# Four token blocks of row fetches become two, and the other two go densely through all experts

## The reference

```python
q = (xt @ wq).reshape(t, 8, 2, 128)
sc = jnp.einsum('thkd,hknd->thkn', q, keys)
s1, i1 = lax.top_k(sc[:, :, 0], 16); s2, i2 = lax.top_k(sc[:, :, 1], 16)
top_s, ci = lax.top_k(all sums s1 + s2, 16)
experts = i1[ci // 16] * 128 + i2[ci % 16]      # 8 heads x 16 of 16384 experts per token
gates = softmax(top_s)
act = gelu(einsum('td,thkd->thk', x, u_tab[experts])) * gates
y = einsum('thk,thkd->td', act, v_tab[experts])
```

## Time and profile before

| | before |
|---|---|
| median of 3 runs | 3802.77 us |
| the profiled execution | 3807.15 us |
| its span | 3805.4 us |
| mean granted TensorE clock | 0.85 |
| PE, DVE, POOL busy | 71%, 54%, 49% |
| moved by DMA | 694.02 MB |
| first expert numbers written (L1278) | at 164.00 us |
| last expert sum added (L1323) | at 1986.33 us |

### The profile page before, as it was taken

One profiled execution on the slowest core, in us unless ns is written; L12 is line 12 of the kernel. 1 busy time (PEld: TensorE's weight loads), 2 busy tenths in 40 slices (PEclk: granted clock), 3 DMA queues, 4 the chain that ended last, 5 costly groups with the idle time before them and its releaser, 6 DMA issues.

```text
span 3805.4 us, 40545 instructions
## 1 busy us (share of the span) xinstructions
...
## 2 busy tenths in 40 slices
...
GB/s 172 128 309 301 279 286 334 321 340 259 313 322 333 310 267 345 332 339 341 356 306 34 67 23 1 1 1 1 56 73 95 89 87 59 23 45 78 95 94 78
DMA packets 417984, 694.02 MB, mean 182 GB/s; under 512 B 35784, under 2 KB 280691, under 8 KB 417667
## 3 DMA queue, kind: packets, MB, share of 16 engines
q0 software_dynamic: 147456, 536.94, 39.7%
q1 hardware_dynamic: 270339, 154.50, 13.9%
...
...
## 4 chain that ended last, share of the span: by engine, by line
PE 51%; DVE 16%; POOL 13%; DMA 10%; issue 6%; ACT 3%; SPq 1%; DVEq 0%; ACTq 0%
PE PS L1593 25%; POOL ring L601 13%; DMA ring<-in_peer_v,eidx 7%; PE PS L768 6%; DMA ring<-in_peer_u,eidx 2%; PE PS L747 2%; DVE ring L1301 2%; PE PS L1495 1%; PE PS L1504 1%; PE PS L653 1%; PE PS L1501 1%; DVE X L1316 1%; PE PS L1603 1%; DVE W L1175 1%; PE PS L1615 1%
## 5 line engine op out<-in xcount | busy, mean ns | idle before, releaser
L601 POOL DMA_INDIRECT ring<-in_peer_u,eidx x512 | 635.8, 1242 | 404.0 <-DVE eidx L1278 177.9
L601 POOL DMA_INDIRECT ring<-in_peer_v,eidx x512 | 588.0, 1148 | 351.4 <-PE PS L768 192.1
L1593 PE MATMUL PS<-held_uH,GW 128*128 128x264 f32 (+1 forms) x3648 | 693.1, 290 | 35.9 <-POOL BIG_value L2120 31.8
L1301 DVE CUSTOM_DVE_ANT_0 ring<-ring,hn 128x1024 f32<-128x1024 f32 x512 | 614.7, 1223 | 115.6 <-DMA ring<-in_peer_u,eidx 106.8
L2106 POOL TENSOR_TENSOR GW<-held_wr,GW 128x1024 fp32r<-128x1024 f32 x178 | 428.6, 2409 | 453.2 <-ACT GW L1883 453.2
L768 PE MATMUL PS<-ring,dg 128*128 128x512 f32 x1024 | 528.2, 655 | 172.4 <-DMA ring<-in_peer_v,eidx 168.0
L1593 PEld LDWEIGHTS PS<-held_uH,GW 128*128 128x128 f32 x3648 | 581.7, 193 | 48.9 <-issue 32.4
L1593 PE MATMUL PS<-BIG_value,GW 128*128 128x264 f32 (+1 forms) x1824 | 486.1, 287 | 0.0
L768 PEld LDWEIGHTS PS<-ring,dg 128*128 128x128 f32 x1024 | 196.2, 206 | 460.6 <-DMA ring<-in_peer_v,eidx 276.6
L1316 DVE SCALAR_TENSOR_TENSOR X<-ring,gact,X 128x1024 f32<-128x1024 f32 x256 | 328.6, 1284 | 186.0 <-DMA ring<-in_peer_v,eidx 181.4
L1593 PE MATMUL PS<-hid,GW 128*128 128x264 f32 (+1 forms) x3072 | 370.4, 282 | 0.0
...
## 6 DMA issues: line engine op xcount, KB each, us to landing
held_wr<-in_w_ff SPq DMA_DIRECT2D x128, 512.0 KB, 4.0
wqr<-in_peer_wq SPq DMA_DIRECT2D x64, 512.0 KB
held_wr<-in_w_in_ab SPq DMA_DIRECT2D x18, 512.0 KB, 3.9
ring<-in_peer_u,eidx POOLq DMA_INDIRECT x512
ring<-in_peer_v,eidx POOLq DMA_INDIRECT x512
BIG<-in_w_in SPq DMA_DIRECT2D x4, 1536.0 KB, 11.4
held_wr<-in_w_qkv_c SPq DMA_DIRECT2D x12, 512.0 KB, 3.8
w_out<-in_w_out SPq DMA_DIRECT2D x1, 4096.0 KB, 19.0
```

What stands on the lines that cost most here:

```text
L601: e.indirect_dma_start(out=ring[:, i % RING, :], out_offset=None, in_=rows_u if k < HK else rows_v, in_offset=bass.IndirectOffsetOnAxis(ap ...
L1301: e.tensor_tensor_reduce(row, row, hn[:, :], 1.0, 0.0, ALU.mult, ALU.add, act[:, k:k + 1]).then_inc(*n.up(e_dot))
L1593: ins = e.matmul(bank[b + a][:, 0:w], w_[:, k * P:(k + 1) * P], x_[:, c0:c0 + w], start=(first and z in (0, 2)), stop=(last and z >= 4))
```

## The change

`first_order()` is written anew. All four fronts come first, one after another, and one expert row of block 0 (a `slot`) follows each of their steps as far as its row is known. Then block 2 and 3, together 256 tokens (`TD`), go through all 16384 experts, with no row fetched by its number:

- `prepare` turns the expert numbers of blocks 2 and 3 into two picks of 0 to 127 (`found`, `picks`), and makes the norms `hs` of both blocks again, transposed and split into high and low parts (`h_hl`).
- 64 `group`s of 4 tokens make the table of gates. For each token DVE writes two 128x128 matrices (first pick; second pick times gate), PE multiplies them, and ACT copies the result into a staging buffer. After every 16 groups SP writes 4 MB of the table to memory (`gates_all`), in runs of 64 floats.
- 128 `tile`s follow, one for each second pick. A tile takes 128 rows of each table, 512 KB each (the first from a transposed copy of the table that the host lays out). ACT casts to the high part and POOL (`low_u`) or DVE subtracts for the low part. PE makes 24 products of 256 columns for the scores, ACT the gelu, DVE multiplies with the tile's gates, and PE makes 24 more products into four banks that gather the sum over all tiles.
- The 256 rows of block 1 are slots between the tiles, 3 after each, with all `v` rows on DVE. The tails of blocks 0 and 1 are put between tiles too; those of 2 and 3 come last, as does the loading of the second transformer block's constants.

Semaphores are merged and some constants moved into a ring buffer to make room. The second transformer block keeps its instructions.

```diff
+GATHERED = (0, 1)
+DENSE = (2, 3)
+TD = P * len(DENSE)
+GROUPS = TD // 4
+STAGE = 64
+FIXED = 149
+def gather_order():
+    for blk in GATHERED:
+        yield "begin", blk
+        for k in range(HK):
+            yield "u", blk, k
+        yield "gate", blk
+        for k in range(HK):
+            yield "v", blk, k
+        yield "end", blk
...
+    rows = list(gather_order())
+    rows.reverse()
+    def ready(name):
+        done = taken.get(("front", name[1]), 0)
+        if name == ("begin", 1):
+            return ("tile", 0) in order
+        if name[0] == "begin":
+            return done >= 40
+        if name[0] == "u":
+            return (done - 35) // 5 > name[2] // TOPK
+        return done == FRONT_STEPS
+    def slots(some):
+        while some and rows and ready(rows[-1]):
+            name = rows.pop()
+            order.append(name)
+            if name[0] in "uv":
+                some -= 1
...
+    fronts += [(("front", b), FRONT_STEPS) for b in range(1, NB)]
     while fronts:
         step(fronts)
-    late = []
-    for b in range(3):
-        late += [(("pproj", b), 1), (("tail", b), TAIL_STEPS)]
-    late.append((("pproj", 3), 1))
-    experts(3, late, (4, 4))
+        slots(1)
+    order.append(("prepare",))
+    for j in range(GROUPS):
+        order.append(("group", j))
+        if j % 2:
+            slots(1)
+    while ready(rows[-1]):
+        slots(1)
+    late = [(("tail", 0), TAIL_STEPS)]
+    for f in range(P + 2):
+        order.append(("tile", f))
+        slots(3)
+        if not rows and taken.get(("tail", 1)) is None and (("tail", 1), TAIL_STEPS) not in late:
+            late.append((("tail", 1), TAIL_STEPS))
+        if f > 8 and f % 3 == 0:
+            step(late)
+    while rows:
+        slots(1)
+    order.append(("sum",))
+    order.append(("second",))
+    if (("tail", 1), TAIL_STEPS) not in late and ("tail", 1) not in taken:
+        late.append((("tail", 1), TAIL_STEPS))
     while late:
         step(late)
-    order += [("tail", 3)] * TAIL_STEPS
...
+    for b in DENSE:
+        order += [("tail", b)] * TAIL_STEPS
...
+        for c in range(TD // STAGE):
+            e.wait_ge(p_ev, STAGE // 4 * (c + 1))
+            e.dma_start(gates_all[:, :, STAGE * c:STAGE * c + STAGE].rearrange("f p t -> p f t"), stage[c % 2]).then_inc(d_go[c % 2], 16)
+        e.wait_ge(d_go[0], 16 * (TD // STAGE // 2))
+        e.wait_ge(d_go[1], 16 * (TD // STAGE // 2))
+        for q in range(3):
+            dense_gates(e, q)
...
+        for f in range(2, P):
+            tables(e, f)
+            if f % 2 == 0 and 3 <= f // 2 + 1 < P // 2:
+                dense_gates(e, f // 2 + 1)
+        e.dma_start(met, ap["meta_tokens_2"]).then_inc(d_p, 16)
         e.wait_ge(t_pT, 1)
         e.dma_start(pin[0], piv[3]).then_inc(d_pin, 16)
+        e.wait_ge(e_x, NB)
+        second_loads(e)
+    def tables(e, f):
+        if f >= 2:
+            e.wait_ge(u_lo, f - 1)
+        e.dma_start(raw_u[f % 2], ap["peer_u_turned"][f].rearrange("p k e -> p (k e)")).then_inc(d_u[f % 2], 16)
+        if f >= 2:
+            e.wait_ge(v_lo, f - 1)
+        e.dma_start(raw_v[f % 2], rows_v.rearrange("(p f) d -> f p d", f=P)[f]).then_inc(d_vt[f % 2], 16)
+    def dense_gates(e, q):
+        if q >= 3:
+            e.wait_ge(a_g, 2 * (q - 3) + 2)
+        e.dma_start(g_ring[:, q % 3], gates_all[2 * q:2 * q + 2].rearrange("f p t -> p f t")).then_inc(d_g[q % 3], 16)
...
+    def low_u(e, n, f):
+        if f < P:
+            e.wait_ge(u_hi, f + 1)
+            e.tensor_tensor(r(u_hl[:, f % 2, 1]), raw_u[f % 2], u_hl[:, f % 2, 0], ALU.subtract).then_inc(*n.up(u_lo))
...
+            elif name[0] == "u":
+                gather(e, 256 * name[1] + name[2] + RING)
+            elif name[0] == "v":
+                gather(e, 256 * name[1] + HK + name[2] + RING)
+            elif name[0] == "tile":
+                if name[1] == 0:
+                    low_u(e, n, 0)
+                low_u(e, n, name[1] + 1)
...
+    def group_tensor(e, n, j):
+        e.wait_ge(p_oh, j + 1)
+        if j >= 2:
+            e.wait_ge(p_ev, j - 1)
+        for i in range(4):
+            ins = e.matmul(bank[1 + j % 2][:, i * P:(i + 1) * P], hot1[:, j % 2, i, :], hot2[:, j % 2, i, :], start=True, stop=True)
+        ins.then_inc(*n.up(p_mm))
+    def score_bank(f):
+        return bank[4 + f % 2][:, 0:TD]
+    def tile_tensor(e, n, f):
+        if f < P:
+            e.wait_ge(u_lo, f + 1)
+            if f >= 2:
+                e.wait_ge(a_gelu, f - 1)
+            for k in range(8):
+                hi, lo = (r(u_hl[:, f % 2, a, k * P:(k + 1) * P]) for a in range(2))
+                x_hi, x_lo = (r(h_hl[:, a, k, :]) for a in range(2))
+                e.matmul(score_bank(f), hi, x_hi, start=(k == 0), stop=False)
+                e.matmul(score_bank(f), hi, x_lo, start=False, stop=False)
+                ins = e.matmul(score_bank(f), lo, x_hi, start=False, stop=(k == 7))
+            ins.then_inc(*n.up(s_mm))
+        g = f - 2
+        if g >= 0:
+            e.wait_ge(v_lo, g + 1)
+            e.wait_ge(a_lo, g + 1)
+            a_h, a_l = (r(a_hl[:, g % 2, a, :]) for a in range(2))
+            for c in range(8):
+                hi, lo = (r(v_hl[:, g % 2, a, c * P:(c + 1) * P]) for a in range(2))
+                dst = bank[c // 2][:, TD * (c % 2):TD * (c % 2) + TD]
+                e.matmul(dst, hi, a_h, start=(g == 0 and c % 2 == 0), stop=False)
+                e.matmul(dst, hi, a_l, start=False, stop=False)
+                ins = e.matmul(dst, lo, a_h, start=False, stop=(g == P - 1 and c % 2 == 1))
+            ins.then_inc(*n.up(y_mm))
...
+    def tail_banks(blk):
+        return (6, 7, 7, 7, 6, 6) if blk in GATHERED else (0, 1, 2, 3, 4, 5)
...
+    def group_scalar(e, n, j):
+        c, i = j // (STAGE // 4), j % (STAGE // 4)
+        if i == 0 and c >= 2:
+            e.wait_ge(d_go[c % 2], 16 * (c // 2))
+        e.wait_ge(p_mm, j + 1)
+        e.copy(stage[c % 2][:, :, 4 * i:4 * i + 4], bank[1 + j % 2].rearrange("p (t f) -> p f t", t=4)).then_inc(*n.up(p_ev))
+    def high_u(e, n, f):
+        if f < P:
+            e.wait_ge(d_u[f % 2], 16 * (f // 2 + 1))
+            if f == 0:
+                for c in range(2):
+                    e.wait_ge(d_go[c], 16 * (TD // STAGE // 2))
+            if f >= 2:
+                e.wait_ge(s_mm, f - 1)
+            e.copy(r(u_hl[:, f % 2, 0]), raw_u[f % 2]).then_inc(*n.up(u_hi))
+    def tile_scalar(e, n, f):
+        if f == 0:
+            high_u(e, n, 0)
+        high_u(e, n, f + 1)
+        g = f - 1
+        if 0 <= g < P:
+            e.wait_ge(s_mm, g + 1)
+            if g >= 2:
+                e.wait_ge(a_lo, g - 1)
+            e.activation(a_raw[:, g % 2], score_bank(g), ACT.Gelu).then_inc(*n.up(a_gelu))
+            e.wait_ge(d_vt[g % 2], 16 * (g // 2 + 1))
+            if g >= 2:
+                e.wait_ge(y_mm, g - 1)
+            e.copy(r(v_hl[:, g % 2, 0]), raw_v[g % 2]).then_inc(*n.up(v_hi))
+            e.wait_ge(a_g, g + 1)
+            e.copy(r(a_hl[:, g % 2, 0]), a_raw[:, g % 2]).then_inc(*n.up(a_hi))
...
+    def renew_hn(e, n, blk):
+        if blk:
+            e.wait_ge(*n.next(f_sq))
+            inverse_root(e, n, sm[:, 5:6], sm[:, 4:5], D)
+            e.wait_ge(*n.now(rinv))
+            e.wait_ge(*n.now(e_dot))
+            e.scalar_tensor_tensor(hn[:, :], X[:, blk, :], sm[:, 5:6], gffn2, ALU.mult, ALU.mult).then_inc(*n.up(dve))
...
+    def group_vector(e, n, j):
+        if j == 0:
+            e.wait_ge(p_T, 1)
+        if j >= 2:
+            e.wait_ge(p_mm, j - 1)
+        for i in range(4):
+            t = 4 * j + i
+            e.tensor_scalar(hot1[:, j % 2, i, :], line[:, :], picks[:, 0, t:t + 1], None, ALU.is_equal)
+            ins = e.tensor_scalar(hot2[:, j % 2, i, :], line[:, :], picks[:, 1, t:t + 1], picks[:, 2, t:t + 1],
+                                  ALU.is_equal, ALU.mult)
+        ins.then_inc(*n.up(p_oh))
+    def tile_vector(e, n, f):
+        g = f - 1
+        if 0 <= g < P:
+            q = g // 2
+            e.wait_ge(a_gelu, g + 1)
+            e.wait_ge(d_g[q % 3], 16 * (q // 3 + 1))
+            e.tensor_tensor(a_raw[:, g % 2], a_raw[:, g % 2], g_ring[:, q % 3, g % 2], ALU.mult).then_inc(*n.up(a_g))
+            e.wait_ge(v_hi, g + 1)
+            e.tensor_tensor(r(v_hl[:, g % 2, 1]), raw_v[g % 2], v_hl[:, g % 2, 0], ALU.subtract).then_inc(*n.up(v_lo))
+            e.wait_ge(a_hi, g + 1)
+            e.tensor_tensor(r(a_hl[:, g % 2, 1]), a_raw[:, g % 2], a_hl[:, g % 2, 0], ALU.subtract).then_inc(*n.up(a_lo))
...
+    ut = np.ascontiguousarray(inputs["peer_u"].reshape(P, P, 8, P).transpose(1, 3, 2, 0))
+    arrays["in_peer_u_turned"] = ut
```

618 lines of the change are left out of this document (363 added, 255 removed).

## The result

The changed kernel takes 4448.35 us, the median of 4 runs (4442.89 to 4458.05), against 3804.08 us of the kernel before beside it. The ratio is 1.169, with a 95% interval of 1.1656 to 1.1724. The direction was forecast, the size was not quite: 4700 us. The range held it. The profiled execution took 4442.89 us, its span 4441.1.

What follows compares the result with a forecast made beforehand. The old kernel's first transformer block was taken as bound by row fetches with DVE close behind, the second by PE. 1040 + 215 + 1580 + 74 + 1788 = 4697, forecast as 4700 us, 24% slower; range 4090 to 4930 us.

Steps and rivals of the forecast that it cites:

- 1. fronts: All four fronts with block 0's rows among their steps, priced by DVE's heads and row costs: ending at 1040 us.
- 2. table of gates: Preparing 25 us, 64 groups of compares on DVE 160 us, last write to memory 30 us: 215 us in sum.
- 3. tiles: 130 turns, 86 at 12.0 us with rows and 44 at 11.2 without, plus 55 us for tail steps and first turn: 1580 us.
- 4. sum and tails: After the tiles: 8 us to bring back the sum, then tails 2 and 3 at 33 us each: 74 us.
- the chain: In the tiles, SP's loads, ACT's cast, POOL's low_u, DVE's gate product and v_lo wait on each other: 11.2 us per turn.
- the turn priced without the lock: In the tiles, if the gate product hid beside POOL's subtraction: 9.9 us per turn, total 4530 us.
- they share the DMA engines ... I add 0.8: In tiles with rows, row fetches share DMA with the tile loads: 0.8 us more per turn, 12.0 for 11.2, over 86 tiles.
- if those without rows take as long as those with: Named sign of being wrong: tiles without rows (forecast 11.2 us) take as long as tiles with rows (12.0 us).
- the rival: In the tiles, rows take half the DMA rate, so a turn with rows takes 14.4 us, total 4900 us; chance 16%.
- the upper end of 64 us: Writing 4.2 MB of gates in 256-byte runs at double the packet time: 64 us, where 30 was taken for the last write.
- Bandwidth, not latency, sets the tile: In the tiles, SP and ACT run far enough ahead for loads to overlap: tiles 977 us, total 4095 us; chance 17%.
- faster than before: Tiles run at PE's pace, 5.7 us, rows included: total 3670 us, breaking even at 6.8 us per tile; chance 3%.

Runs made afterwards that it cites:

- e2: Changed kernel with SP issuing the load of u(f+1) ahead of v(f), so u no longer stands behind the wait for v_lo: 4010.21 us, ratio 1.051.
- e3: Changed kernel with the subtraction low_u moved from POOL to DVE, ahead of the gate product: 4325.70 us, ratio 1.135.
- x1: Changed kernel with one of three PE products left out for scores and y, 32 of 48 per tile: 4433.20 us, ratio 1.164.
- e5: Changed kernel with the rows of block 1 (but one) behind the last tile, none among the tiles: 4825.47 us, one run.
- e4: Changed kernel with both the edits of e2 and e3: 3936.11 us, ratio 1.033.
- e9: e7 with one wait less at the first cast, plus two block 0 rows behind each of a front's first 36 steps: 3897.61 us, ratio 1.021.
- e7: e4 with nine rows of block 1 per four tiles instead of twelve, and the tails' weights loaded behind the tiles' loads: 3898.12 us, ratio 1.022.
- e11: e7 with one wait less, merged compares and u(2) loaded earlier, plus rows shifted earlier into the fronts, fewer in the tiles: 3876.06 us, ratio 1.019.

## Why the prediction came out as it did

By its own steps, against the profiled execution of after:

| | forecast us | measured us |
|---|---|---|
| 1. fronts | 1040 | 1021 |
| 2. table of gates | 215 | 160 |
| 3. tiles | 1580 | 1414 |
| 4. sum and tails | 74 | 69 |
| second block | 1788 | 1777 |
| sum | 4697 | 4441 |

**The mechanism was right but for the rows' share.** Every link of the chain stands in the trace in the forecast order, e2 shows that the queue's order closes it, e3 that POOL's subtraction stretches the gate product, x1 and e5 that PE and the rows have next to no share. The lock that the Trainium skill describes ("SBUF — State Buffer", "SBUF: two separate sides") is borne out again: 2.28 us beside POOL, 0.42 in e3. That the turn priced without the lock was 9.9 us, and that of e3 is 9.93, is partly luck: the price was for another chain, through the gelu and ACT's cast of `v`, where that of e3 goes through `low_u` on DVE, and it had 6.0 us for the loads, which take 5.7 on average in after. One sign was misjudged: PE was to sit idle for half of each tile, and is 69 to 73% busy. The text priced its products at the full clock, and the tiles were granted 0.81 to 0.83.

**The sizes were too high in four terms of part 3**, 166 us in sum.
- "they share the DMA engines ... I add 0.8": rows cost nothing that could be told from zero, 11.00 us with and 10.96 without. Over 86 tiles that is 69 us. The text named "if those without rows take as long as those with" as a sign of being wrong, and it is what happened: here the mechanism was wrong, not only the size. The step gives no row for its 0.8. The only row on contention is in the rival, a transfer of 4 MB beside a full ring (24.3 us); in the tiles DMA is 73% busy, and e5 moves less than half as much per us at the same turn.
- The turn itself: 5.2 us from `v_lo` to the cast without gates and 6.2 with, where 5.6 and 6.4 were priced (no view parts this into the load of `v` and what `u` adds), and 4.9 for the rest where 5.2 were. The tail steps, priced at 30 us, are inside the measured mean of 10.98. Together (11.2 - 10.98) x 125 + 30 = 57 us.
- The first turn is 24.65 us, where 11.2 + 25 were priced, 12 us.
- The last four turns were priced like all, 45 us. No load is awaited there, and the pipeline drains in 16.9 us: 28 us.

**Part 2** was 55 us too high. A pair of compares takes 116 / 256 = 0.45 us and not 0.62, since each starts before the last has ended: the durations of 0.34 and 0.28 overlap. That makes 44 us. The last write took 20.7 us for 30, and the preparing 21 for 25; some 2 us lie between the last compare and the write. The write was priced at 31 ns per packet, the mean of the queue before. It took 18: 0.91 of 20.75 us on 16 engines for 16384 runs. On the short writes the rule of the Trainium skill ("DMA: Bandwidth & Descriptors", Specifications) made the upper end of 64 us the likelier one. The writes do miss the rate, 4.19 MB in 20.7 us is 203 GB/s where e4 moves 382, but they cost a third of that end. No run writes the same bytes in longer runs, so that their length is the cause is not shown.

**Part 1** was 19 us too high. A head with 5 `u` rows takes 14.77 us, forecast 15.8; in e9 a bare head takes 9.4, so a row between two steps of the front costs 1.08 us and not 1.31: it stands partly in the gaps of the dependent steps.

**The second block** took 1777 us for 1788, 11 of the 256 us, with the same instructions. PE was busy 1605 us in it and 1617 in the kernel before, granted 0.94 and 0.93. In other versions it took 1771 (e4) to 1788 (e7), so a difference of this size comes from execution to execution, whatever the change. What makes it is open.

**The rivals.** "Bandwidth, not latency, sets the tile" is false for this kernel and became true two edits later. The argument against "faster than before" was that no slice of before shows 404 GB/s. Slices of e4 reach 399, and it holds 382 for 605 us. The highest slice of a profile is what that kernel asked for, not what the engines give. Still, 404 was not held by any version, and with three rows to a tile the turns of e4 took 7.07 us on average, over the 6.8 of breaking even. In the kernel after, the chain never asked for such a rate.

**Why dense is slower at all.** Most of the 17% is the chain: with it cut, 3.3% are left in e4. What follows on the rest is an argument from the profiles; no run tests it by itself. In e7 the DMA engines, nearly full in the tiles, move 184 GB/s on average in the fronts, 111 in the gates and hardly anything in the 75 us of the end. The kernel before kept them at 87 to 91%, in most slices from the fourth on over 300 GB/s, and so moved its 99 MB more (694.02 against 594.72) in less time. At its 355 GB/s those 99 MB are 280 us. The fronts and gates of e7, 1160 us at 111 to 184 GB/s, lose by the same rate an estimated 590 us. And e9 and e11 show that rows put there lengthen the fronts, so this time can't simply be filled.
